# Per-head sums of squares: one fp32 product, or two products with the high and the low part of the squares

## What is computed

```python
def rms_norm_2(x, g):
    xf = x.astype(jnp.float32)
    y = xf * lax.rsqrt(jnp.mean(xf * xf, axis=-1, keepdims=True) + RMS_EPS)
    return (y * g.astype(jnp.float32)).astype(x.dtype)
...
    h = rms_norm_2(x, mix_norm)
    proj = h @ w_in
    idx = np.cumsum(IN_SPLITS)[:-1].tolist()
    dq, dk, dv, fq, fk, fv, g_dil, g_diff = jnp.split(proj, idx, axis=-1)

    gshape = (B, S, N_DIL_GROUPS, DIL_HEADS, HEAD_DIM)
    dq = apply_rope(rms_norm_2(dq.reshape(gshape), dil_q_norm), cos, sin)
    dk = apply_rope(rms_norm_2(dk.reshape(gshape), dil_k_norm), cos, sin)
```

## Time and profile before

| | |
|---|---|
| median of 3 runs | 3446.45 us (3443.82 to 3447.12) |
| the profiled execution's own time | 3442.34 us |
| its span, first to last instruction | 3440.6 us |
| PE busy | 3397.8 us (99%) |
| DVE busy | 2241.4 us (65%) |
| ACT busy | 1726.3 us (50%) |
| POOL busy | 563.9 us (16%) |
| mean granted clock of PE | 0.996 |

### The profile page before, as it was taken

The page is one execution under the profiler, slowest core; times in us unless marked ns, Lnnn a source line. Parts: engine busy times, 40 slices in busy tenths (PEclk is TensorE's granted clock), DMA queues, the critical chain, the costliest instruction groups (busy, mean ns, idle before and its releaser), DMA issues.

```text
span 3440.6 us, 58872 instructions
## 1 busy us (share of the span) xinstructions
PE 3397.8 (99%) x19482; PEld 2956.2 (86%) x19482; DVE 2241.4 (65%) x2932; ACT 1726.3 (50%) x2550; POOL 563.9 (16%) x509
## 2 busy tenths in 40 slices
PE   8999999999999999999999999999999999999999
PEld 7888878888888878888888888888888888888888
DVE  7757677777754465655555588855687655565544
ACT  5444565555544454454444444454566554445443
POOL 1203111111100011111100057711110111111000
PEclk9999999999999999999999999999999999999999
DMA  6423545555556645555566655554556555555665
GB/s 200 153 95 117 177 151 185 190 188 186 191 187 188 188 151 191 187 189 186 190 183 191 203 178 179 174 179 156 165 194 195 190 189 186 192 186 189 186 189 171
DMA packets 175309, 616.09 MB, mean 179 GB/s; under 512 B 20832, under 2 KB 21248, under 8 KB 174848
## 3 DMA queue, kind: packets, MB, share of 16 engines
q1 hardware_dynamic: 173936, 607.67, 54.4%
q10 hardware_dynamic: 1296, 7.41, 0.6%
HBM read 610.81 MB, written 4.19 MB: 179 GB/s over the span
## 4 chain that ended last, share of the span: by engine, by line
PE 86%; DVE 9%; issue 2%; ACT 1%; DMA 1%; POOL 0%; SPq 0%; DVEq 0%; ACTq 0%; POOLq 0%
PE acc L353 55%; PE acc L356 27%; DVE weights_low L279 3%; DVE x_T L2453 1%; DVE x_T L2451 0%; ACT weights_high L272 0%; DVE arena L2457 0%; PE ps_narrow L2195 0%; PE ps_wide L2171 0%; DVE x_T L2455 0%; DVE arena L426 0%; DVE x_T L2461 0%; DVE moving_halves L579 0%; DVE x_T L685 0%; DVE x_T L2445 0%
## 5 line engine op out<-in xcount | busy, mean ns | idle before, releaser
L353 PE MATMUL acc<-moving_halves,weights_high 128*128 128x512 f32 x6400 | 2049.3, 401 | 3.8 <-DVE weights_low L279 3.1
L279 DVE TENSOR_TENSOR weights_low<-weights_raw,weights_high 128x1024 fp32r<-128x1024 f32 (+1 forms) x1184 | 1437.4, 1228 | 742.6 <-ACT weights_high L272 741.1
L272 ACT ACTIVATE weights_high<-weights_raw 128x1024 fp32r<-128x1024 f32 (+1 forms) x1184 | 1220.6, 1033 | 797.3 <-PE acc L356 775.5
L356 PEld LDWEIGHTS acc<-moving_halves,weights_low 128*128 128x128 f32 x6400 | 1205.3, 188 | 284.2
L356 PE MATMUL acc<-moving_halves,weights_low 128*128 128x256 f32 x6400 | 1260.7, 278 | 0.0
L353 PEld LDWEIGHTS acc<-moving_halves,weights_high 128*128 128x128 f32 x6400 | 982.6, 189 | 21.9 <-issue 15.0
L353 PE MATMUL acc<-gated_halves,weights_high 128*128 128x512 f32 x2112 | 663.5, 395 | 0.0
L420 ACT ACTIVATE cross_products<-acc 128x256 f32<-128x256 f32 x512 | 195.6, 382 | 696.4 <-PE acc L356 696.3
L356 PEld LDWEIGHTS acc<-gated_halves,weights_low 128*128 128x128 f32 x2112 | 396.8, 188 | 93.7
L443 POOL TENSOR_TENSOR stage_scratch<-unscaled,token_scale 128x256 f32<-128x256 f32 x264 | 218.8, 829 | 1288.5 <-DVE unscaled L426 786.2
L356 PE MATMUL acc<-gated_halves,weights_low 128*128 128x256 f32 x2112 | 415.1, 278 | 0.0
(11 more groups left out here) (339 smaller groups left out, 1848.0 us busy)
## 6 DMA issues: line engine op xcount, KB each, us to landing
weights_raw<-in_w_in SPq DMA_DIRECT2D x272, 512.0 KB, 3.9
weights_raw<-in_ffn_up SPq DMA_DIRECT2D x176, 512.0 KB, 4.0
weights_raw<-in_ffn_w_gate SPq DMA_DIRECT2D x176, 512.0 KB, 3.7
weights_raw<-in_ffn_w_up SPq DMA_DIRECT2D x176, 512.0 KB, 4.3
weights_raw<-in_ffn_w_down SPq DMA_DIRECT2D x160, 512.0 KB, 3.9
weights_raw<-in_ffn_down SPq DMA_DIRECT2D x80, 512.0 KB, 4.1
weights_raw<-in_w_out SPq DMA_DIRECT2D x64, 512.0 KB, 3.8
weights_raw<-in_ffn_w_down SPq DMA_DIRECT2D x32, 256.0 KB, 2.7
```

Source lines behind the costliest of these rows:

```text
L272: core.nc.scalar.activation(core.high[:, slot, 0:nk, :].rearrange("p a b -> p (a b)"), core.raw[:, slot, 0:nk * P], ACT.Copy).then_inc(cor ...
L279: core.nc.vector.tensor_tensor(core.low[:, slot, 0:nk, :].rearrange("p a b -> p (a b)"), core.raw[:, slot, 0:nk * P], core.high[:, slot, 0 ...
L353: core.nc.tensor.matmul(acc[:, t % 2, :, :], core.high[:, u % SLOTS, k, :], parts[:, prod.first[t] + k0 + k, :, :], start=(k0 + k == 0), s ...
L356: core.last = core.nc.tensor.matmul(acc[:, t % 2, 0, :], core.low[:, u % SLOTS, k, :], parts[:, prod.first[t] + k0 + k, 0, :], start=False ...
```

## The change

ACT writes the squares twice: once in fp32 as before, and once rounded to `F32R` (`head_squares_high`). DVE subtracts the second from the first and writes the difference, rounded to `F32R`, over the fp32 squares (`head_squares_low`). PE multiplies the ones (copied once to `F32R` before body 1) with the high part and then with the low part, into the same bank. PE no longer waits for ACT's squares but for DVE's subtraction, which has its place at tile 0, ahead of the taking of that tile. The three tiles lie in parts of the memory of x that this stage has free.

```diff
@@ mix_in_stage: scalar @@
         act.wait_ge(kept, 16)
+        nc.scalar.activation(ones, core.c("ones"), ACT.Copy).then_inc(squared, 1)
 
         def head_step(i, t):
             if t == 0:
                 taken(core, act, prod, i - 1, 1)
                 nc.scalar.activation(sq, pair(i - 1), ACT.Square).then_inc(squared, 1)
+                nc.scalar.activation(sq_high, pair(i - 1), ACT.Square).then_inc(squared, 1)
@@ vector @@
+        def squares_low(i):
+            dve.wait_ge(squared, i * 2 + 1)
+            nc.vector.tensor_tensor(sq_low, sq, sq_high.bitcast(F32), ALU.subtract).then_inc(own, 1)
...
         for body in range(1, QK_BODIES):
             for i, t in walk(body, body + 1):
-                if t == 1:
+                if t == 0:
+                    squares_low(i)
+                else:
                     variance(i)
                 take_head(i, t)
                 if t == 1:
                     normalize(i)
@@ tensor @@
             if t == 0:
-                pe.wait_ge(squared, i)
-                nc.tensor.matmul(p_sq[:, :, :], core.c("ones"), sq, start=True, stop=True).then_inc(summed, 1)
+                pe.wait_ge(own, i * 4 - 3)
+                nc.tensor.matmul(p_sq[:, :, :], ones, sq_high, start=True, stop=False)
+                nc.tensor.matmul(p_sq[:, :, :], ones, sq_low, start=False, stop=True).then_inc(summed, 1)
```

More of the change, by code:

```diff
@@ L141, in __init__ @@
         self.h_at = nc.sbuf_base
+        self.x_at = self.h_at - KT * S * 4
         self.h_mem = self.sb("halves_memory", [P, KT, 2, S], F32)
@@ L2350, in mix_in_stage @@
     var, tmp, swap, root, sq = (core.x[:, 2 * j:2 * j + 2, :] for j in (1, 2, 3, 5, 6))
+    sq_high, sq_low, ones = (core.over(core.x_at + 4 * S * j, name, 1)[:, 0, :, :] for j, name in (
+        (0, "head_squares_high"), (12, "head_squares_low"), (14, "ones_high")))
+    ones = ones[:, 0, 0:P]
     token_eps = core.total[:, :]
@@ L2451, in normalize @@
             nc.vector.tensor_tensor(tmp, root, root, ALU.mult).then_inc(own, 1)
-            dve.wait_ge(own, i * 3 - 2)
+            dve.wait_ge(own, i * 4 - 2)
             nc.vector.scalar_tensor_tensor(tmp, tmp, -0.5, var, ALU.mult, ALU.mult).then_inc(own, 1)
-            dve.wait_ge(own, i * 3 - 1)
+            dve.wait_ge(own, i * 4 - 1)
             nc.vector.scalar_tensor_tensor(root, tmp, 1.5, root, ALU.add, ALU.mult).then_inc(own, 1)
-            dve.wait_ge(own, i * 3)
+            dve.wait_ge(own, i * 4)
             nc.vector.scalar_tensor_tensor(here, here, core.v("head_gain", i - 1), root, ALU.mult, ALU.mult).then_inc(normed, 1)
```

## The result

The changed kernel takes 3541.0 us (median of 4 runs, 3538.4 to 3542.2) against 3446.5: ratio 1.0275, 95% interval 1.0257 to 1.0293. It is 94.5 us slower, the forecast was 85 with a range of 54 to 112.

What follows compares the result with a forecast made beforehand. PE was taken to bound the kernel, at 12.01 us a body; the new PE-DVE loop makes 14.88 + 1.67 = 16.55. Over the bodies, with end terms, +86.8 us gives 3529.1 to 3533.3, written as 3531, range 3500 to 3558.

Steps and rivals of the forecast that it cites:

- Products 0.40 shorter: On PE, two new products take 0.46 us against 0.86 for the old: 0.40 saved in each of 20 bodies.
- the rival of the wait that is met: Subtraction ends before PE is through with tile 0, so only the 8.0 us saving remains: 3438 us; chance 0.04.
- ACT's second square at no cost: ACT's added square of 0.62 us lies beside DVE's work: cost 0; if late, 0.62 a body.
- Variance to subtraction 8.13: On DVE, from variance to the subtraction's place in the queue at tile 0: 8.13 us, a loop link.
- Subtraction 0.68: DVE's new subtraction on two 128x512 fp32 operands takes 0.68 us, from a row without contention.
- Hand-over to PE 0.33: From the end of DVE's subtraction to PE's start: 0.33 us, taken from body 20's variance wait.
- Product to variance 5.74, plus 1.67 for the clock: Last loop link, PE's product to DVE's next variance: 5.74 us, plus 1.67 lost to the lower clock after PE idles.
- GpSimd's meeting with the split: DVE's next split comes upon POOL's last rotation operation, period 15.12 instead of 14.88; drops out with the clock's fall.
- 2.87 + 81.7: Added time: 2.87 us from body 1 to 2, without rotation or clock fall, and 81.7 over 18 further bodies, 4.54 each.
- the clock holds: Rival: PE's clock doesn't fall behind the short idle stretches: 3506 us, or 3501 without POOL's meeting; chance 0.22.
- the low clock lasts longer: Rival: PE's low clock lasts as after 4.26 us idle, 2.8 us lost a body: 3555 us; chance 0.16.
- GpSimd holds up the refinement: Rival: GpSimd's rotation keeps delaying the root's refinement, 18 x 0.98 = 17.6 us on top: 3551 us; chance 0.05.

Runs made afterwards that it cites:

- the filled kernel: The changed kernel with 12 more short products on PE, result unread, after tile 0 ahead of the wait in bodies 1 to 20: 3517.9 us, ratio 1.0215.
- wait only: The kernel before, old product kept, no second square or subtraction; DVE copies 8 numbers per partition in the subtraction's place and PE waits for that: 3504.6 us.
- the kernel with the products alone: The changed kernel without the subtraction: both short products read the high part, PE waits for ACT's squares: 3443.1 us, ratio 0.9994.
- both orders: Changed kernel with early squares and the subtraction behind normalize's second operation, 3450.6 us; the same with ACT's cross copy ahead of the reciprocal root, 3452.2 us.

## Why the prediction came out as it did

The forecast was right in sign and mechanism, and 10 us low (3531 against 3541). Step by step, with the numbers of the change's profile:

- *Products 0.40 shorter.* 0.46 for the two, as said, where PE doesn't wait ahead of them; behind the new wait it is 0.57, at the full clock too (the filled kernel). The saving is 0.39 there as well: at the full clock it is 6.19 from product to variance with the old product ("wait only") and 5.80 with the two new ones. That each 0.40 would show in the time if nothing waited ("only the 8.0 us would remain", the rival of the wait that is met) was wrong: the kernel with the products alone gains nothing that can be measured. I had read "DVE busy 87.41 of 100" as slack. Its round, idle gaps for ACT's root included, was 11.95 against PE's 12.01.
- *ACT's second square at no cost.* Right for the change: there nothing waits for it in the stage. In the kernel with the products alone PE waited for it twice.
- *Variance to subtraction 8.13.* 8.12.
- *Subtraction 0.68.* This is the term that was mis-sized: 1.77 in 15 bodies, 15 x 1.09 = 16.4 us. I took the duration from a row without contention, and had GpSimd's first operation wait until DVE paused, as in the earlier trace rows. The kernel without rotation shows that GpSimd is the cause; that its operation gets in ahead of the subtraction is how I read the timelines.
- *Hand-over to PE 0.33.* It is 0.05 to 0.06 (2074.66 + 1.77 = 2076.43, PE at 2076.48); 19 x 0.27 = 5.1 us too much. The row of body 20 that it came from is another wait, at another place of PE's program; there it is 0.33 in the changed kernel too (variance ends at 2322.85, PE starts at 2323.18). Why it is longer there isn't shown.
- *Product to variance 5.74, plus 1.67 for the clock.* 7.36 in most bodies, 7.15 to 7.29 in four. Against the 5.80 of the filled kernel, 1.56 for the clock, which was thus 0.11 too much, and the rest 0.06 too little. For the link as a whole, 7.41 against 7.36, that is 18 x 0.05 = 0.9 too much, and in the four bodies another 0.6. It fell in every body from 2 on. That the clock had held in 300 to 302 was weak ground for "a shorter one did no harm": the idle stretch in it is that of 2.24 in the list at the end, and behind the same stretch the clock did fall in the profiled run of the change.
- *GpSimd's meeting with the split.* Absent with the clock's fall, as forecast; in the filled kernel, where the clock holds, it shows once, in the one body with a short subtraction: 6.18 from product to variance, and 16.12 instead of 15.76 to the next product.

The 19 distances from the first product to the last had 2.87 + 81.7 = 84.6 us in the forecast. 84.6 + 16.4 - 5.1 - 0.9 - 0.6 is 94.4, for 94.1 on the trace. Outside them the forecast had another 2.2 (0.89, 1.67 and -0.40), of which the trace shows nothing: PE waits 0.36 ahead of the first product, and from the last one to the end it is 1225.4 us against 1226.0.

Part of the agreement is luck: the hand-over and the last link were 6.6 us too long, and that hides as much of the 16.4 us that were missing. Of the 94.5 us the kernels give 60 to the wait in that place, with a clock that falls in 10 of 19 bodies, and 65.8 to the whole change without GpSimd's rotation. The last 29 come with GpSimd: 16.4 for the longer subtraction, and 9 x 1.56 = 14.0 because the clock then falls in all 19 bodies and not in 10. The rule of the Trainium skill, "TensorE: Matmul & The Clock Gate", section "Why this matters for your kernels", held for the change: the idle stretches between bursts brought the lower clock. The section speaks of longer gaps than some that brought it here: behind 2.23 us and behind 2.8 us the clock fell in 10 of 19 bodies each, and there the measurement decides. Behind the 1.14 of the filled kernel it stayed at 1.00.

The rival "the clock holds" (3506) fell with the 0.90; "the low clock lasts longer" (3555) with the 1.56; "GpSimd holds up the refinement" did not come (its operations take 0.68 and 0.69 in bodies 1 to 19), but the same contention came at the subtraction, where no rival had it.

## What to carry to other kernels

When a change gives a waiting engine a new producer, compare two times before any durations: when the producer's queue reaches the new instruction, and when the waiter needs it. If the first is later, and the producer's next round depends on the waiter, the lateness doesn't wear off: each round takes the length of the whole loop, here 5.3 us more a body for 0.4 saved. An engine's slack isn't its idle share; it is what the length of its round, with the waits in it, leaves of the bottleneck's round (here 12.01 - 11.95).

## What the hardware showed that I had not expected

- An operation of GpSimd seems to go ahead of one of DVE's that is next in line. The subtraction took 0.67 or 1.77, nothing between; the 1.1 more is a little under one operation of GpSimd's (1.28 alone), and without the rotation it is gone. The two splits just ahead of it were 2.33 in each of bodies 2 to 20.
- The same idle stretch on PE is not always followed by the same clock. Behind 3.85 us it was the lower one in all 15 bodies of the change, behind 2.75 in all four; behind the 2.8 of the kernel without rotation and the 2.23 of "wait only" in 10 of 19; behind 1.14 never. The stretch of 2.24 us in the earlier trace rows, from which I had taken that a short one does no harm, stands in a stage that no kernel here changes. The kernel before, then the change:

```profile
301.64 0.63 PE L1456 MATMUL ps_narrow<-constants,arena 128*128 128x128 f32 x4 [2.24 <-DVE arena L1911]
```

```profile
305.79 1.08 PE L1457 MATMUL ps_narrow<-constants,arena 128*128 128x128 f32 x4 [2.23 <-DVE arena L1912]
```

The 24 matmuls behind it take 3.7 us in three of the 13 traces, that of before among them, and 5.2 to 5.3 in the other ten. A single row where the clock held was chance. What decides it isn't shown.
- Filling DVE's idle time didn't shorten its round: 12.43 in both orders, with about 0.6 moved from idle time to a longer operation.
